# 160 gathered tokens instead of 128, and the gates of six blocks moved ahead, in a transformer trunk on one core

## The reference

```python
def expert_block(args):              # 128 tokens at a time
    hx, ix, gx = args                # tokens, their 128 chosen experts of 16384, their gates
    act = jax.nn.gelu(jnp.einsum('tkd,td->tk', u[ix], hx), approximate=False) * gx
    return jnp.einsum('tk,tkd->td', act, v[ix])
```

## Time and profile before

| | us |
|---|---|
| median of 3 runs (lowest, highest) | 3934.22 (3932.24, 3934.82) |
| the profiled execution: its own time | 3937.54 |
| its span in the trace | 3935.9 |
| PE busy | 3843.4 (98%) |
| DVE busy | 2832.6 (72%) |
| POOL busy | 1745.8 (44%) |
| ACT busy | 1902.5 (48%) |

### The profile page before, as it was taken

The page is one execution under the profiler, slowest core; times in us unless marked ns, Lnnn a source line. Parts: engine busy times, 40 slices in busy tenths (PEclk is TensorE's granted clock), DMA queues, the critical chain, the costliest instruction groups (busy, mean ns, idle before and its releaser), DMA issues.

```text
span 3935.9 us, 60526 instructions
## 1 busy us (share of the span) xinstructions
PE 3843.4 (98%) x18901; PEld 3304.5 (84%) x18901; DVE 2832.6 (72%) x5565; ACT 1902.5 (48%) x3593; POOL 1745.8 (44%) x1769
## 2 busy tenths in 40 slices
PE   8998999999999899999999999999999999999998
PEld 6665888888888899999788888888888887999997
DVE  3747799778732588886777773998777623888876
ACT  3746433577743333334555553333877633333334
POOL 0311345778720588841200001446877602788711
PEclk9999999999999999999999999999999999999999
DMA  8557566555556699993588873334555655999972
GB/s 268 168 154 184 163 200 205 196 194 190 187 213 205 224 370 372 370 369 123 158 239 240 236 213 113 115 119 154 201 190 187 235 194 173 334 366 363 374 254 91
DMA packets 547145, 875.96 MB, mean 223 GB/s; under 512 B 40576, under 2 KB 384768, under 8 KB 543136
## 3 DMA queue, kind: packets, MB, share of 16 engines
q1 hardware_dynamic: 458544, 605.81, 47.2%
q0 software_dynamic: 51568, 201.04, 13.9%
q10 hardware_dynamic: 36864, 67.13, 4.6%
HBM read 745.57 MB, written 262.21 MB: 256 GB/s over the span
## 4 chain that ended last, share of the span: by engine, by line
PE 72%; POOL 14%; issue 6%; DVE 3%; ACT 3%; DMA 1%; ACTq 0%; another core or an unknown queue 0%; DVEq 0%; POOLq 0%
PE ps L188 64%; POOL own_act L1546 6%; POOL own_rows L1556 6%; PE ps L1706 2%; ACT first_scaled L1725 1%; POOL w_lo L174 1%; PE ps L2243 1%; PE ps L2222 1%; DMA own_rows<-value_rows,own_row_at 1%; ACT w_hi L161 1%; PE ps L1208 1%; PE ps L2013 1%; DVE w_lo L167 1%; PE ps L929 0%; PE ps L570 0%
## 5 line engine op out<-in xcount | busy, mean ns | idle before, releaser
L188 PE MATMUL ps<-h_hi,w_hi 128*128 128x512 f32 (+1 forms) x3072 | 1157.9, 377 | 32.5 <-DVE w_lo L167 12.9
L167 DVE TENSOR_TENSOR w_lo<-w_raw,w_hi 128x1024 fp32r<-128x1024 f32 x584 | 718.2, 1230 | 631.4 <-ACT w_hi L161 595.5
L188 PE MATMUL ps<-h_hi,w_lo 128*128 128x512 f32 (+1 forms) x3072 | 1143.9, 372 | 1.4 <-issue 1.4
L188 PE MATMUL ps<-h_lo,w_hi 128*128 128x512 f32 (+1 forms) x3072 | 1143.0, 372 | 0.6 <-issue 0.6
L161 ACT ACTIVATE w_hi<-w_raw 128x1024 fp32r<-128x1024 f32 x693 | 733.1, 1058 | 801.0 <-PE ps L188 599.5
L188 PE MATMUL ps<-y_hi,w_hi 128*128 128x512 f32 (+1 forms) x2368 | 873.2, 369 | 17.7 <-DVE w_lo L167 13.2
L188 PE MATMUL ps<-y_hi,w_lo 128*128 128x512 f32 (+1 forms) x2368 | 869.1, 367 | 1.2 <-issue 1.2
L188 PE MATMUL ps<-y_lo,w_hi 128*128 128x512 f32 (+1 forms) x2368 | 868.4, 367 | 1.1 <-issue 0.9
L188 PEld LDWEIGHTS ps<-h_hi,w_hi 128*128 128x128 f32 x3072 | 578.5, 188 | 128.5 <-issue 23.0
L188 PEld LDWEIGHTS ps<-h_hi,w_lo 128*128 128x128 f32 x3072 | 578.2, 188 | 83.5 <-issue 1.5
L188 PEld LDWEIGHTS ps<-h_lo,w_hi 128*128 128x128 f32 x3072 | 578.6, 188 | 80.0 <-issue 3.9
(11 more groups left out here) (359 smaller groups left out, 3613.4 us busy)
## 6 DMA issues: line engine op xcount, KB each, us to landing
value_rows<-in_v SPq DMA_DIRECT2D x256, 512.0 KB, 6.0
w_raw<-in_u SPq DMA_DIRECT2D x256, 512.0 KB
w_raw<-in_v SPq DMA_DIRECT2D x256, 512.0 KB
acts<-gelu ACTq DMA_DIRECT2D x256, 256.0 KB, 2.2
gates<-gate_group POOLq DMA_DIRECT2D x28, 2048.0 KB, 8.0
gelu_block<-acts SPq DMA_DIRECT2D x256, 192.0 KB
gate_block<-gates SPq DMA_DIRECT2D x96, 512.0 KB
w_raw<-in_od_in SPq DMA_DIRECT2D x65, 512.0 KB
```

The lines of the kernel that those rows point to most:

```text
L167: self.nc.vector.tensor_tensor(self.wl[:, slot % SPL, :], self.raw[:, slot, :], self.wh[:, slot % SPL, :].bitcast(F32), ALU.subtract).then ...
L188: ins = self.nc.tensor.matmul(out, a[:, s, w], b[:, k, :], start=first and j == 0 and m == 0, stop=last and j == n - 1 and m == 2)
```

## The change

The number of tokens with gathered rows goes from 128 to 160: the last 128 as before, and the 32 before them (EXTRA). Those 32 are laid four times over the 128 partitions, 32 of their 128 experts on each quarter, so they add 32 values of `k` (K = 160). At the end a matmul with `quad` adds the four quarters. The dense part works on DT = 352 columns instead of 384. Gates still builds the gates of 384 tokens (GT), so nothing is removed there.

The products of activations and gates are done in pieces of four tiles (QUAD) instead of one. For blocks 2, 3, 4, 5, 0 and 1 (GATED) they are moved into the tail beside the `u` units: SP fetches the blocks there, DVE multiplies, blocks 0 and 1 stay on the chip, and the products of blocks 2 to 5 are written back to `acts` (`put_back`) and fetched again later without gates. TURNS is now twelve `k` per block in blocks 0 to 3, starting behind unit 5, and eleven per block from block 4 on (LATER). LEAD is 12, and activations meet their own gates in groups of 8 instead of 16.

```diff
-DT = T - P
+GT = T - P
+EXTRA = 32
+DT = GT - EXTRA
...
-    K = PEER_HEADS * SEL
-    GROUP = 16
+    KA = PEER_HEADS * SEL
+    KB = KA * EXTRA // P
+    K = KA + KB
+    GROUP = 8
     RING = 4
-    LEAD = 24
-    FIRST = 1
-    TURNS = (1, 1, 1, 2, 1, 1, 1, 2)
+    LEAD = 12
+    FIRST = 5
+    TURNS = (2, 2, 1, 2, 1, 1, 1, 2)
+    LATER = (1, 2, 1, 2, 1, 1, 1, 2)
+    TURN_AT = 4
...
+        for k in range(own.LEAD):
+            own.load_act(pool, k)
         for i in range(NBLOCK):
-            s = i % 2
             for j in range(B):
-                if i == 0:
-                    for k in range(j * per, j * per + per):
-                        own.load_act(pool, k)
                 for k in own.turns(i, j):
                     own.load_act(pool, k + own.LEAD)
                     own.load_row(pool, k + own.RING)
...
+    def put_back(self, sp, m, h):
+
+        n, b, s = self.QUAD, self.GATED[m], m % 2
+        sp.wait_ge(self.pre.sem, self.pre.at(m * BLOCK + (h + 1) * n))
+        first = b * BLOCK + h * n
+        sp.dma_start(self.rows.acts[first:first + n, :, 0:DT].rearrange("n p t -> p n t"),
+                     self.at[:, s, h * n:h * n + n, :]).then_inc(self.put[h].sem, 16)
...
+    def make(self, dve, i, s, j):
+
+        n, half = self.QUAD, BLOCK // 2
+        if 2 <= i < len(self.GATED) and j == 0:
+            dve.wait_ge(self.bl[s].sem, self.bl[s].at(self.landed(i)))
+            dve.sem_inc(self.gt_.sem, BLOCK)
+        if i >= len(self.GATED) and j < half and j % 2 == 0:
+            self.mult(dve, i, s, j * n // 2)
+        if j >= half and j % 2 == 0:
+            self.lo(dve, i, s, (j - half) * n // 2)
...
-                ins.then_inc(used.sem, 1)
+                    w = slice(j * P, (j + 1) * P)
+                    p.nc.tensor.transpose(p.ps[:, j, GT:T], own.sum[:, 0, w], p.ident[:, :])
+                    ins = p.nc.tensor.matmul(p.ps[:, j, DT:GT], own.sum[:, 1, w], p.quad[:, :], start=True, stop=True)
+                ins.then_inc(used.sem, 1)
```

More of the change, by code:

```diff
@@ L277, in _ @@
                                     fill=0.0, base=-1, pattern=[[-1, P]], channel_multiplier=1)
-    const.base += 1
+    const.base += 2 + P // EXTRA
+    for k in range(DK):
+        p.sig(f"x_loaded{k}").base += 16
     ld.base += 16
@@ L1431, in tensor @@
         for k in range(3):
-            for t in range(DT // P):
+            for t in range(GT // P):
                 ins = p.nc.tensor.transpose(p.ps[:, 2 + k, t * P:(t + 1) * P],
@@ L1498, in vector @@
-        v.tensor_copy(own.gate[:, :], key[:, 2, mine])
-        v.tensor_copy(own.row_at[:, :], expert)
-        link(v.tensor_copy(own.act_at[:, :], place))
+        own, last = self.own, GT // P
+        expert, place = self.expert[:, 0:2, :], self.expert[:, 2:4, :]
+        for n in range(2):
+            mine = slice((last - n) * S, (last - n + 1) * S)
+            link(v.scalar_tensor_tensor(out=expert[:, n, :], in0=key[:, 0, mine], scalar=float(KEYS),
+                                        in1=key[:, 1, mine], op0=ALU.mult, op1=ALU.add))
+            link(v.scalar_tensor_tensor(out=place[:, n, :], in0=expert[:, n, :], scalar=float(T),
+                                        in1=p.token[:, n:n + 1].to_broadcast([P, S]), op0=ALU.mult, op1=ALU.add))
@@ new lines, in vector @@
+        v.tensor_copy(own.gate[:, 0:S], key[:, 2, last * S:(last + 1) * S])
+        v.tensor_copy(own.row_at[:, 0:S], expert[:, 0, :])
+        v.tensor_copy(own.act_at[:, 0:S], place[:, 0, :])
+        for g in range(P // EXTRA):
+            to, of = slice(g * EXTRA, (g + 1) * EXTRA), slice(P - EXTRA, P)
+            some, base = slice(g * own.KB, (g + 1) * own.KB), (last - 1) * S
+            v.tensor_copy(own.gate[to, S:own.K], key[of, 2, base + g * own.KB:base + (g + 1) * own.KB])
+            v.tensor_copy(own.row_at[to, S:own.K], expert[of, 1, some])
+            ins = v.tensor_copy(own.act_at[to, S:own.K], place[of, 1, some])
@@ L1773, in blocks, with landed, fetch @@
         body(NBLOCK - 1, 1, NBLOCK - 1, None)
-    def fetch(self, sp, i, s, j, again):
+    def landed(self, i, m=None):
+        if m is None:
+            m = len(self.GATED) - 2 + i % 2
+            late = [16 * BLOCK if k < len(self.GATED) else self.PER for k in range(2 + i % 2, i + 1, 2)]
+        else:
+            late = []
+        return self.PER * (m // 2 + 1) + sum(late)
+    def put_back(self, sp, m, h):
[4 more added lines that the diff above has]
+                     self.at[:, s, h * n:h * n + n, :]).then_inc(self.put[h].sem, 16)
+    def fetch(self, sp, i, s, j, again, gates=True):
         B, at, gt = BLOCK, self.at, self.gt
@@ L1817, in gpsimd @@
         pool.wait_ge(own.rows.done.sem, own.rows.done.at(16 * KEYS))
+        for h in range(2):
+            pool.wait_ge(self.put[h].sem, self.put[h].at(16 * self.TRIPS))
         for k in range(own.RING):
@@ L1846, in lo, with his @@
-    def lo(self, dve, i, s, j):
-        dve.wait_ge(self.ah.sem, i * BLOCK + self.ah.base + j + 1)
-        self.p.nc.vector.tensor_tensor(self.dense[s][1][:, j, :], self.at[:, s, j, 0:DT],
-                                       self.dense[s][0][:, j, :].bitcast(F32), ALU.subtract
-                                       ).then_inc(self.al.sem, 1)
-    def early(self, k):
-        per = BLOCK // self.AHEAD
-        first = (k - (self.TAIL - self.AHEAD)) * per
-        return range(first, first + per) if first >= 0 else ()
+    def his(self, act, i, s, j):
+        for k in range(*self.HI_AT[j:j + 2]):
+            self.hi(act, i, s, k)
@@ L1907, in vector @@
             p.split_lo(dve, u, u % RAW)
-            for j in self.early(k):
-                self.mult(dve, 0, 0, j)
-                if j:
-                    self.lo(dve, 0, 0, j - 1)
+            m, h = divmod(k - self.FETCH_AT - 2, self.STEPS)
+            if 0 <= m < len(self.GATED) and h < 2:
+                self.mult(dve, self.GATED[m], m % 2, h * self.QUAD, m)
+            if k >= self.TAIL - BLOCK:
+                self.make(dve, 0, 0, k - self.TAIL + BLOCK)
         for i in range(NBLOCK):
@@ L2577, in ffn @@
         with ExitStack() as outer:
[L2578 removed]
+            b["sel"] = p.sb("selected", [P, 4, GT + Gates.TK], ctx=outer)
             b["gates"] = p.sb("gate_group", [P, 2, KEYS, TG], ctx=outer)
```

166 lines of the change are left out of this document (94 added, 72 removed).

## The result

| | before | after |
|---|---|---|
| median of 4 runs, us | 3933.77 | 3998.24 (3987.27 to 4017.3) |
| ratio, 95% interval | | 1.0169 [1.0123, 1.0215] |
| profiled execution, its span | 3935.9 | 3986.6 |
| stretch of 128 `v` units, layer 1 / 2 | 559.3 / 559.6 | 575.5 / 594.0 |

A forecast was written before the change was run, and what follows sets the result against it. POOL's gathers were taken to bound Values: 296 at 1.68 us plus the other terms give 590.4 us per layer, +61.9 us over two, nothing elsewhere, so 3999.4 us (median 3996). Range 3918 to 4060, with 70% on 3960 to 4045.

The forecast's parts named there:

- The pace: Values: POOL's gathers, not PE, set the time from block 1 to block 13, without a pause, at 1.63 to 1.76 us.
- waits for adds in the middle: Sign that the forecast is wrong: POOL waiting for adds in the middle of Values, or a period under 1.58.
- Its sum: Values, one layer: 19.2 + 8 + 497.3 + 7.4 + 57.5 + 1 = 590.4 us, against 559.3 and 559.6.
- The period: Time from one POOL gather to the next in Values: 1.68 us taken, between two rules; bounds 1.25 and 1.80.
- the random meeting: Gathers meet DVE instructions at random; mean wait is half the squared durations over the time: periods 1.76 and 1.67.
- The share rule: A gather's wait goes with DVE's busy share alone: periods 1.70 and 1.63 us in Values.
- The opening: Block 0 of Values: PE's loss of 17 us halved to 8 with a run half as long; bounds 0 and 17.
- PE: Values: matmuls 0.1598 us apart instead of 0.1733; 41.6 us less per layer, 83 over two if PE were the bound.
- Tail, Decode, start: Parts outside Values, all priced at nothing; tail's DMA share near 0.9, SP's new waits bounded at 0 and 10 us per layer.
- Rival A: Values: gathers keep up at 1.4 us or less, PE stays the bound, 3836 to 3851 us; 5%.
- rival B: Values: the period falls less far; break-even 1.576 us, at 1.50 the kernel takes 3889 us; 13%.
- Rival C: Values: PE idles between units and its clock drops to 1.2 GHz; 20 to 60 us more, 4020 to 4060; 12%.

The follow-up runs named there:

- e2_rows: Changed kernel without the activation gathers from k = 24 on (add k uses activation k mod 24): 3856.1 us, ratio 0.9889 to the kernel before.
- a0_again: The changed kernel run once more, unaltered, in a group where the kernel before took 3898.2 us: 3938.54 us, ratio 1.0106.
- e3_fetch: Changed kernel with SP's fetches of a block's piece set back by two units, behind two more weight loads: 3944.49 us, ratio 1.0115 to the kernel before.
- e4_small: Changed kernel with DVE's pieces of four tiles cut into single ones at the same places: 3896.79 us, ratio 0.9998 to the kernel before.
- e5_both: Changed kernel with single-tile DVE pieces and SP's fetches set back by two units: 3904.16 us, ratio 1.0015 to the kernel before.
- e7_quads: Kernel before, with products and low parts in DVE pieces of four tiles at the changed kernel's places: 3883.62 us, ratio 0.9962.
- e1_cols: Kernel before, with dense products of blocks 1 to 15 of Values on 352 columns instead of 384: 3864.01 us, ratio 0.9908.
- e11_even_back: e4_small with k spread evenly (four per three units), LEAD 7, GROUP 4, and SP's fetches set back: 4000.93 us, ratio 1.0164 to the kernel before.
- e7_again: The kernel of e7_quads run again, in a group where the kernel before took about 3939.0 us: 3948.7 us, ratio 1.0015.

## Why the prediction was right, and where it was off

**The pace.** Right in the first layer, in part in the second. POOL's gathers set the time of the changed kernel: hardly a pause in layer 1 from 1500 to 1720 us (2.8 us), DVE's wait for rows up from 48.4 to 112.5 us in the whole run, and e2_rows gives 82 us back when half of the gathers go. But the prediction named waits for adds in the middle as a sign that it is wrong, and in layer 2 they stand there: 36.2 us from 3345 to 3500, where late releases hold DVE and not POOL's pace. At the low level they are gone (0.6 us from 1352 to 1685 in a0_again), and POOL's pace holds throughout. Its sum, 85.1 + opening + 296 periods, holds with the measured period (counted from 70 us behind a stretch's start to 110 us before its end) in all kernels with these turns and all gathers:

| stretch | period | opening | sum | measured |
|---|---|---|---|---|
| after, layer 1 / 2 | 1.626 / 1.701 | 8 | 574 / 597 | 575.5 / 594.0 |
| a0_again | 1.614 / 1.608 | 0 | 563 / 561 | 562.4 / 556.5 |
| e3_fetch | 1.604 / 1.621 | 0 | 560 / 565 | 561.7 / 562.3 |
| e4_small | 1.519 / 1.530 | 0 | 535 / 538 | 537.5 / 540.3 |
| e5_both | 1.553 / 1.542 | 0 | 545 / 542 | 548.1 / 543.5 |

The period is counted inside the stretch that it is compared with, with POOL's waits in it. So the table bears out the terms beside it (296 gathers, 85.1 us around them), and not a reason for the period.

**The period** is the term that was mis-sized. 1.68 was taken; the mean of the two layers is 1.66, but by two causes. POOL's own pace is 1.61 to 1.64 us (layer 1 and a0_again); by it a layer takes some 575 us. The 594 of layer 2 has late releases in it (56.8 us of them behind block 0, 27.8 in layer 1), which the sum priced in the opening alone. The two errors nearly cancel, 61.9 us forecast and 50.7 in the profiled execution; without the second, at the low level, the same form gives 40. That the number fits to a tenth of a per cent is luck in this respect. The step that failed is the carrying over of the random meeting: e7_quads shows that the mean wait does not follow the sum of squares. (Its sum for the first blocks is also off: 12 adds, 8 splits and 2 long pieces give 36.9 and a period of 1.69, not 35.2 and 1.67.) The share rule gives 1.70 and 1.63 and was nearer here, but e7_quads refutes it as well. What holds is the single case, for a gather that is held: it ends 0.81 to 0.82 us behind the DVE instruction that it meets. What both rules miss is how many are held: 168 of 194 in the kernel before, 110 of 205 in the changed one, 107 of 208 in a0_again, 142 of 219 in e4_small, 114 of 195 in e7_quads. It goes with what stands where in DVE's stream, and that was not worked out.

This also decides the point that was open between the Trainium skill and the trace, page "SBUF — State Buffer", section "Who interferes with whom". Its inference that `tensor_tensor` leaves descriptor generation alone doesn't hold in this case: the gather of 2.37 us above met a `tensor_tensor`, and cutting such pieces took 42 us off the kernel. In the kernel before, 78 of the 79 gathers that met a `tensor_tensor` from 1352 to 1685 us ended 0.81 to 0.84 us behind it.

**The opening.** Taken at 8 us; the first blocks took 39.2 and 38.6 us instead of 30.7, so 8.5 and 7.9. At the low level it is 0. It goes with the late releases (11.2 us in block 0 of each layer), not with the length of the run of activation gathers, by which the prediction halved it: at the low level a run of 12 costs nothing (a0_again), nor does one of 24 (e1_cols and e7_quads, whose first blocks take PE's 33.3 us). That the half came out right is luck.

**PE.** Right: the spacing is 0.16 us,

```profile
1349.69 0.32 PE L192 MATMUL ps<-h_hi,w_hi 128*128 128x352 f32 x1
1349.85 0.32 PE L192 MATMUL ps<-h_lo,w_hi 128*128 128x352 f32 x1
```

and e1_cols shows that the kernel before could use only 35 of these 78 us as well.

**Tail, Decode, start.** Right: at nothing. The stretches start at 1283.7 (1284.0 before), and the second starts 16.9 us later, of which 16.2 are the first stretch. The tail's estimate of the DMA share, near 0.9, was 0.96 to 0.99, and SP's new waits didn't reach PE, which stands at 100.00 of 100 us.

**Rival A and B** are out: the break-even of 1.576 was missed by 0.03 to 0.05 us at the least. e4_small is what rival B would have been, 1.52. At the low level the kernel before loses nothing in the opening either, as far as e1_cols and e7_quads tell; with 559.3 - 17 = 542.3 us for its stretch (an estimate) its break-even there is lower, (542.3 - 85.1) / 296 = 1.545, and 1.52 comes out as no change.

**Rival C** happened in part. PE stood at the 1.2 GHz level for 34.1 and 54.6 us of the stretches, against 17.1 and 13.7 before, behind idle gaps of up to 3.1 and 4.8 us. A price can't be told from the scatter: e3_fetch has 34.1 and 37.5 us of it, a0_again 13.7 and 23.9, and their layers differ by -0.7 and +5.8 us.

**What stays open**: why PE's count `w_used` rises late at the high level, and what sets the level. It costs the kernel before 36 us (its first blocks are 17.5 and 15.5 us over PE's 33.3), the changed kernel 60. It isn't SP's order (e11_even_back), nor a full DMA: it occurs at a DMA share of 0.18 and of 0.85. PE also halts inside the product that runs during the longest wait (0.98 us before 3458.49, with nothing to wait for by the trace), so the cause may lie in PE's own stream. Whether it has to do with the semaphore records that are missing at the same level wasn't tested.

## What to carry to other kernels

Where GpSimd issues gathers without a pause, as here, its time per gather goes by what VectorE does at their start (0.94 us beside an idle one, 2.37 behind a product of four tiles): price an edit of VectorE's stream by it, not by VectorE's busy time, and measure how many gathers are held and for how long, since meetings aren't random. Before a wait is put down to a late load, look when the load was issued and whether its queue moves anything; the waiting instruction may need a second semaphore. Shortening the engine that looks 97% busy pays only down to the pace of the next one; work out both paces per block before moving work from one to the other. When the same kernel shows two levels on different occasions, compare only within an occasion, and try a candidate at both.

## What was not expected of the hardware

- Fewer, longer VectorE instructions can shorten GpSimd's gathers (1.41 to 1.24 and 1.21 us at the high level, e7_again; 1.18 at the low one, e7_quads) and can lengthen them (1.21 to 1.30, e4_small against a0_again); both are nearly the same work.
- A gather that meets a two-input VectorE instruction isn't always held: from 1352 to 1685 us of a0_again 21 of 208, begun within 0.08 us of the start of an add or a split, took 0.94 us.
- The same program at two levels: 3883.6 and 3948.7 us for e7_quads and e7_again, with 0 and 73 us of late releases in the two stretches.
- A semaphore that PE counts up rose 10.5 us after the matmul that counts it had ended in the records (3455.09 and 3465.60), while the weights that ScalarE was thought to wait for had long landed.
